# RWKV passes: TensorE products from the gram to the last inverse level as tiles of 32 columns in place of 64

## The chip, the cores and the metric

The kernel runs on one core of one Trainium2 chip. The metric is the device time in microseconds. The kernel before takes 2187.87 us (median of two runs, 2187.61 and 2188.13).

The core's engines are PE (TensorE; PEld is its weight load), DVE (VectorE), ACT (ScalarE), POOL (GpSimd) and SP, which issues DMAs.

## What is computed

Two blocks follow each other on 512 tokens of width 1024, all in float32. The first mixes a gated convolution and a forgetting attention and ends in a feed-forward part. The second puts 16 meta tokens ahead (528 tokens), runs an RWKV-7 mixer and then a latent attention. The change lies in the RWKV mixer:

```python
r, k, v, g, w_lo, a_lo = jnp.split(h, ...)            # h = [x, dx] @ w_comb, 32 heads of 64
def step(S, inp):
    r_t, w_t, k_t, v_t, a_t, b_t = inp
    sa = jnp.einsum('bhij,bhj->bhi', S, a_t)
    S = S * w_t[:, :, None, :] + sa[..., None] * b_t[:, :, None, :] + v_t[..., None] * k_t[:, :, None, :]
    return S, jnp.einsum('bhij,bhj->bhi', S, r_t)
```

The recurrence over tokens is not run token by token: it is cut into chunks of 64 tokens, and within a chunk a unit triangular system is solved.

## The kernel before

The 32 heads are worked off as 16 pairs (`PAIRS`); the two heads of a pair lie on partitions 0 to 63 and 64 to 127 (`own[0]`, `own[1]`). The tokens, padded to 576, make 9 chunks (`NC_`) of `C` = 64. A pass `i` is a software pipeline over three pairs:

- A, pair `i`: the projections of r, k, v and g. Each of 8 items (four kinds by two token halves of 264) is 8 steps (`KD`) of a contraction over 1024 channels; a step is one `fill`. It issues one product for each of the two column halves `own` of the pair: weights `raw_k` of 128 rows x 64 columns, 264 streamed columns, into two halves of the partitions of a PSUM bank (L1446).
- B, pair `b = i - 1`: the gram products (L1650, weights of 64 rows x 128 columns) and the inverse of the triangular systems of the nine chunks, by squaring in levels 1 to 5. A level makes x = mb' t (L1661, `x_mm`), which DVE evicts to `x_m` (L2036), and then t' = t x (L1677, at the last level L1679, `tt_mm`), which DVE adds to `t_m` (L2042). Each product of a chunk streams 64 columns against 64 weight columns for each of the two heads. The chunks go in two parts (4 and 5, or 3 and 5 from level 4 on), so that DVE works on one while PE works on the other.
- C, pair `c = i - 2`: the scan over the chunks (L1569 to L1621).

Beside these, `head_sums` (L1707) sums squares over a head's 64 channels with a matrix of ones: four products of 264 streamed columns, called in the inverse by `ssk` (level 3) and `gn_var` (level 4) and behind it by `bonus`.

The order on each engine is written out by hand. On PE, `fill(k)` draws the next k projection steps between the dependent products, by the tables `FILL_GRAM` = 7, `FILL_FIRST` = 5, `FILL_X` = (2, 2, 2, 2, 2) and `FILL_T` = (2, 2, 1, 0, 1): 28 steps from the gram to the end of the inverse. Passes with an inverse are i = 1 to 16; those with projections are i = 0 to 15. In pass 16 the fills are steps of the output projection instead (`wo_unit`, L161 to L163, weights of 128 x 128).

Of the kernel before, what the change touches and what calls it, by code (L numbers as in the profile page):

```python
# [37 lines left out]
C = 64  # L38
# [32 lines left out]
def program(nc, io, out):  # L71
    with ExitStack() as base:
# [27 lines left out]
        ps = base.enter_context(nc.psum_tensor("ps", [P, 8, 512], F32))  # L100
# [1220 lines left out]
        mb = put("mb", [P, NC_, P])  # L1321
        tb = put("tb", [P, NC_, P])
        rb = put("rb", [P, NC_, P])
        t_m = put("t_m", [P, NC_, C])
        x_m = put("x_m", [P, NC_, 2, C])
        t_t = put("t_t", [P, NC_, C])
# [55 lines left out]
        def parts_of(lv):  # L1382
            return PARTS if lv < 4 else LAST_PARTS
        own = [slice(C * h, C * h + C) for h in range(2)]

        SCAN_FILLS = [(1, 2, 2), (1, 1, 1)] + [(1, 1, 2)] * (NC_ - 3) + [(1, 1, 2)]
        FILL_TURN, FILL_GRAM, FILL_FIRST, FILL_END = 1, 7, 5, 0
# [8 lines left out]
        def ge(eng, s, v):  # L1396

            if not (isinstance(v, int) and v <= 0):
                eng.wait_ge(s, v)
# [21 lines left out]
        def item_out(n):  # L1421
            bank, at = ITEM_AT[n]
            return ps[:, bank, at:at + T2 // 2]
# [5 lines left out]
        def projection(pe, i, n):  # L1429

            kind, h = ITEMS[n]
            dst = item_out(n)
            t = "rkvg".index(kind)
            cols = slice(h * (T2 // 2), (h + 1) * (T2 // 2))
            before = [m for m in range(n) if ITEM_AT[m][0] == h]
            if before:
                pe.wait_ge(a_ev, 12 * i + (before[-1] + 1))
            else:
                ge(pe, a_ev, 12 * i - 1)
            if h == 0:  # L1440
                pe.wait_ge(rw_landed[t % 2], 32 * i + (16 * (t // 2) + 16))
            for k in range(KD):
                if i == 0 and h == 0:
                    pe.wait_ge(mx_done, KD * t + k + 1)
                for m in own:
                    mm = nc.tensor.matmul(dst[m, :], raw_k[t % 2][:, k, m], mixed[t][:, k, cols], start=(k == 0), stop=(k == KD - 1))  # L1446
                if k == KD - 1:

                    mm.then_inc(a_mm, 1)
                yield  # L1450
# [96 lines left out]
        def pass_pe(pe, i, A, B, Cs):  # L1547
# [10 lines left out]
            def fill(k):  # L1558

                for _ in range(k):  # L1560
                    next(steps, None)
# [11 lines left out]
            def p_product(n):  # L1573

                for h in range(2):
                    mm = nc.tensor.matmul(ps[own[h], 2, 0:C], gm[:, n, 1, own[h]], uv[:, n, h, :], start=True, stop=True)  # L1576
                mm.then_inc(p_mm, 1)
            if Cs:
                pe.wait_ge(rb_ev, 2 * c + 2)
            for n in range(NC_):  # L1580
# [24 lines left out]
                if Cs:  # L1605
                    pe.wait_ge(p_ev, 9 * c + (n + 1))
                    for h in range(2):
                        mm = nc.tensor.matmul(ps[own[h], 2, C:P], tb[:, n, own[h]], p_sb[:], start=True, stop=True)  # L1608
# [4 lines left out]
                if Cs:  # L1613
# [5 lines left out]
                    if n < NC_ - 1:  # L1619
                        for h in range(2):  # L1620
                            mm = nc.tensor.matmul(ps[own[h], 3, C:P], bk_rows[:, n, own[h]], uv[:, n, h, :], start=(n == 0), stop=True)  # L1621
# [6 lines left out]
            if B:  # L1628

                pe.wait_ge(fa, 14 * b + FA["v"])  # L1630
                pe.wait_ge(pa, 13 * b + PA["bkb"])
                if A:
                    pe.wait_ge(a_ev, 12 * i + LORA)
                else:
                    for x in range(NC_):
                        if x % 8 == 0:
                            pe.wait_ge(yy_ev, 2 * c + (x // 8 + 1))
                        for h in range(2):
                            mm = nc.tensor.matmul(ps[own[1 - h], 5 + x // 8, C * (x % 8):C * (x % 8) + C], rkv[:, x, 2 * C:3 * C],
                                                  cent[:, own[h]], start=True, stop=True)  # L1640
                    mm.then_inc(turn_mm, 1)
                fill(fill_turn)
                if not A:
                    pe.wait_ge(rows_turned, TURNED * b + (NC_ - 1 + 2))
                elif Cs:
                    pe.wait_ge(yy_ev, 2 * c + 2)
                for q, (c0, m) in enumerate(TURNS):
                    for x in range(m):
                        for h in range(2):
                            mm = nc.tensor.matmul(ps[:, 2 + 3 * h + q, x * P:x * P + P], bk[own[h], c0 + x, :],  # L1650
                                                  rkv[own[h], c0 + x, 0:2 * C], start=True, stop=True)
                    mm.then_inc(g_mm, 1)
                fill(fill_gram)
                for lv in range(1, 6):
                    for p, (c0, m) in enumerate(parts_of(lv)):
                        if lv == 1:
                            pe.wait_ge(mb_ev, 4 * b + (2 * p + 2))
                        pe.wait_ge(tm_ev if lv == 1 else tadd_ev, 2 * b + (p + 1) if lv == 1 else 8 * b + (2 * (lv - 2) + p + 1))
                        for x in range(m):
                            for h in range(2):  # L1660
                                mm = nc.tensor.matmul(ps[own[h], 2 + p, x * C:x * C + C], mb[:, c0 + x, own[h]], t_m[:, c0 + x, :],  # L1661
                                                      start=True, stop=True)
                        mm.then_inc(x_mm, 1)
                        if lv == 1 and p == 0:
                            fill(fill_first)
                    fill(fill_x[lv - 1])
                    for p, (c0, m) in enumerate(parts_of(lv)):
                        pe.wait_ge(x_ev, 10 * b + (2 * (lv - 1) + p + 1))
                        if lv == 1:
                            pe.wait_ge(t0_ev, 6 * b + (2, 6)[p])  # L1670
                        else:
                            pe.wait_ge(tb_ev, 8 * b + (2 * (lv - 2) + p + 1))
                        for x in range(m):
                            for h in range(2):
                                dst = ps[own[h], 4 + p, x * C:x * C + C]
                                if lv < 5:
                                    mm = nc.tensor.matmul(dst, t_t[:, c0 + x, :], x_m[:, c0 + x, h, :], start=True, stop=True)  # L1677
                                else:
                                    mm = nc.tensor.matmul(dst, x_m[:, c0 + x, h, :], t_t[:, c0 + x, :], start=True, stop=True)  # L1679
                        mm.then_inc(tt_mm, 1)  # L1680
                    fill(fill_t[lv - 1])
                    if lv == 3 and A:
                        ssk(pe, i)
                    if lv == 4 and Cs:
                        gn_var(pe, i, c, A)
                pe.wait_ge(kkgm_ev, 2 * b + 2)
                pe.wait_ge(state0, 4 * b + (4 if A else 2))
                p_product(0)
                if A:
                    bonus(pe, i, Cs, c)  # L1690
                fill(fill_end)
            else:
                fill(25 if A else 8)
                if A:
                    ssk(pe, i)
                    fill(8)
                if Cs:
                    pe.wait_ge(wo_ev, 2 * EARLY)
                    gn_var(pe, i, c, A)
                    fill(16)  # L1700
                if A:
                    bonus(pe, i, Cs, c)

        def head_sums(src):
            for h in range(2):
                for m in own:
                    mm = nc.tensor.matmul(ps[m, 6 + h, 0:T2 // 2], halves_ones[:, m], src(h), start=True, stop=True)  # L1707
            return mm

        def ssk(pe, i):  # L1710
            pe.wait_ge(fa, 14 * i + FA["sq"])
            head_sums(lambda h: token_cols(sq_b, h)).then_inc(ssk_mm, 1)

        def gn_var(pe, i, c, A):
            pe.wait_ge(ysq_ev, c + 1)
            if A:
                pe.wait_ge(ssk_out, i + 1)
            head_sums(lambda h: ysq_b[:, h * (T2 // 2):(h + 1) * (T2 // 2)]).then_inc(var_mm, 1)

        def bonus(pe, i, Cs, c):  # L1720
            pe.wait_ge(pa, 13 * i + PA["rr"])
            if Cs:
                pe.wait_ge(gn_ln, c + 1)
            else:
                pe.wait_ge(ssk_out, i + 1)
            head_sums(lambda h: token_cols(rr_b, h)).then_inc(bon_mm, 1)
# [1193 lines left out]
        with nc.Block() as block:  # L2920
# [77 lines left out]
            def _(pe):  # L2998
                front_pe(pe)
                all_passes(pe, pass_pe, x2_under=False)  # L3000
                def squares_of(slot, h):
                    at, cols = HALVES2[h]
# [290 lines left out]
```

## Time and profile before

| | us |
|---|---|
| median of the runs | 2187.87 |
| span of the profiled execution | 2182.5 |
| PE busy | 2151.9 (99%) |
| PE weight load busy | 1730.7 (79%) |
| DVE / POOL / ACT busy | 1287.0 (59%) / 1199.3 (55%) / 829.3 (38%) |
| L1446 (projections), four kinds | 146.5 + 144.0 + 137.6 + 125.4 |
| L1661 (x of the inverse) | 96.9 |
| L1677 (t of the inverse) | 77.3 |

The profile is of one execution. Its span goes from the first to the last instruction; the time of a run also takes in what lies around it. A record of PE is a MATMUL instruction from the start of its reading to a modelled end, so records overlap and their mean duration is not what each adds to the time: for that, read where one run of records starts and where the next does. A form such as "128*64 128x264 f32" is rows*columns of the weights and partitions x elements streamed.

### The profile page before, as it was taken

The numbers are of one execution on the slowest core, as the hardware profiler recorded it, in microseconds if no ns is written. First come the engines' busy times: TensorE is split into PE (matmuls) and PEld (weight loads), VectorE is DVE, ScalarE is ACT, GpSimd is POOL, SyncE is SP. The second block draws the span as 40 slices with busy tenths as digits, with TensorE's granted clock in tenths as the row PEclk, the third lists the DMA queues.
The fourth block names the chain that finished last, engine by engine and source line by source line (L and its number), as shares of the span: only waits on it lengthen the run. The fifth ranks groups of instructions, "written<-read, shape, count | busy, mean of one in ns | idle before, by whom it ended". The sixth has DMA issues, their size and how long they took to land.

```text
span 2182.5 us, 49885 instructions
## 1 busy us (share of the span) xinstructions
PE 2151.9 (99%) x20695; PEld 1730.7 (79%) x20695; DVE 1287.0 (59%) x2558; ACT 829.3 (38%) x1712; POOL 1199.3 (55%) x843
## 2 busy tenths in 40 slices
PE   8999999999999999999999999999989999999999
PEld 6888888788888767777777777777879788888877
DVE  5465467977850766666666666666531476656521
ACT  4122212333320354555555555555411345444410
POOL 5555567788766163555545555555636443443455
PEclk9999999999999999999999999999999999999999
DMA  4323323333332143333333333333624322212132
GB/s 130 87 77 85 80 88 96 93 98 98 98 108 97 42 124 77 87 95 89 90 93 98 90 101 105 90 90 90 196 71 125 107 69 63 66 53 57 54 127 95
DMA packets 368490, 200.80 MB, mean 92 GB/s; under 512 B 124411, under 2 KB 348793, under 8 KB 367881
## 3 DMA queue, kind: packets, MB, share of 16 engines
q1 hardware_dynamic: 368074, 197.53, 32.3%
q8 instruction: 166, 2.72, 0.5%
q14 instruction: 59, 0.48, 0.1%
q10 hardware_dynamic: 191, 0.07, 0.0%
HBM read 162.69 MB, written 22.04 MB: 85 GB/s over the span
## 4 chain that ended last, share of the span: by engine, by line
PE 92%; DVE 3%; POOL 2%; ACT 1%; issue 1%; DMA 0%; SPq 0%; DVEq 0%; POOLq 0%; ACTq 0%
PE ps L1446 21%; PE ps L161 16%; PE ps L163 16%; PE ps L162 16%; PE ps L1661 4%; PE ps L1677 3%; PE ps L1707 2%; PE ps L1650 2%; PE ps L2722 2%; PE ps L1621 1%; PE ps L1576 1%; PE ps L1608 1%; PE ps L1569 1%; PE ps L2706 1%; PE ps L1464 1%
## 5 line engine op out<-in xcount | busy, mean ns | idle before, releaser
L152 POOL TENSOR_TENSOR w_lo<-raw,w_hi 128x1024 fp32r<-128x1024 f32 (+1 forms) x163 | 416.6, 2556 | 13.6
L149 POOL TENSOR_SCALAR w_hi<-raw 128x1024 fp32r<-128x1024 f32 (+1 forms) x163 | 182.2, 1118 | 397.1 <-PE ps L163 380.9
L161 PE MATMUL ps<-h_hi,w_hi 128*128 128x512 f32 x616 | 242.2, 393 | 2.8 <-DVE h_lo L1129 1.7
L163 PE MATMUL ps<-h_hi,w_lo 128*128 128x512 f32 x616 | 240.0, 390 | 0.0
L162 PE MATMUL ps<-h_lo,w_hi 128*128 128x512 f32 x616 | 239.9, 389 | 0.0
L1446 PE MATMUL ps<-mixed_k,raw 128*64 128x264 f32 x1024 | 146.5, 387 | 0.0
L1446 PE MATMUL ps<-mixed_r,raw 128*64 128x264 f32 x1024 | 144.0, 387 | 0.2 <-ACT ws_b L1741 0.2
L161 PEld LDWEIGHTS ps<-h_hi,w_hi 128*128 128x128 f32 x616 | 115.7, 188 | 28.6 <-DVE h_lo L1129 2.8
L1446 PE MATMUL ps<-mixed_g,raw 128*64 128x264 f32 x1024 | 137.6, 387 | 0.0
L163 PEld LDWEIGHTS ps<-h_hi,w_lo 128*128 128x128 f32 x616 | 115.7, 188 | 24.5
L162 PEld LDWEIGHTS ps<-h_lo,w_hi 128*128 128x128 f32 x616 | 115.8, 188 | 22.9
L1144 DVE SCALAR_TENSOR_TENSOR up_c<-up_raw,params,up_c 128x512 f32<-128x512 f32 x88 | 119.0, 1357 | 20.3 <-ACT up_c L862 18.7
L1446 PE MATMUL ps<-mixed_v,raw 128*64 128x264 f32 x1024 | 125.4, 388 | 0.0
L2036 DVE TENSOR_TENSOR x_m<-ps,lv_pad 128x640 f32<-128x640 f32 (+2 forms) x160 | 110.8, 726 | 16.4 <-PE ps L1661 11.9
L1661 PEld LDWEIGHTS ps<-t_m,mb 128*64 128x64 f32 x2752 | 96.1, 138 | 15.2 <-DVE t_m L2042 0.4
L1661 PE MATMUL ps<-t_m,mb 128*64 128x64 f32 x2752 | 96.9, 222 | 0.2 <-DVE t_m L2042 0.2
L1446 PEld LDWEIGHTS ps<-mixed_v,raw 128*64 128x64 f32 x1024 | 71.0, 137 | 31.4
L1979 DVE COPY uv<-ps 64x64 f32<-64x64 f32 x160 | 34.8, 218 | 94.6 <-PE ps L1608 94.1
L161 PE MATMUL ps<-z_both,w_hi 128*128 128x264 f32 x256 | 80.7, 315 | 6.9 <-POOL w_lo L2095 5.9
L2827 ACT ACTIVATE xT<-ps,nmax 128x144 f32<-128x144 f32 (+1 forms) x64 | 34.6, 541 | 135.6 <-DVE nmax L2865 135.4
L1677 PEld LDWEIGHTS ps<-x_m,t_t 128*64 128x64 f32 x2240 | 76.7, 138 | 10.5 <-DVE x_m L2036 0.6
L1758 ACT ACTIVATE uv<-ps 64x64 f32<-64x64 f32 x128 | 27.9, 218 | 146.7 <-PE ps L1608 146.7
(494 smaller groups left out, 5823.5 us busy)
## 6 DMA issues: line engine op xcount, KB each, us to landing
raw<-in_rwkv_w_in_dram SPq DMA_DIRECT2D x64, 512.0 KB, 4.4
raw<-in_w_up_dram SPq DMA_DIRECT2D x44, 512.0 KB, 3.9
raw<-in_w_in_dram SPq DMA_DIRECT2D x41, 512.0 KB, 3.9
raw<-in_w_down_dram SPq DMA_DIRECT2D x22, 512.0 KB, 3.5
raw<-in_mla_w_in_dram SPq DMA_DIRECT2D x22, 512.0 KB, 4.0
sb_kept<-xT SPq DMA_DIRECT2D x16, 528.0 KB, 2.7
xT<-sb_kept SPq DMA_DIRECT2D x16, 528.0 KB, 4.5
raw<-in_rwkv_w_out_dram SPq DMA_DIRECT2D x16, 512.0 KB, 4.4
```

What stands on the lines that cost most here:

```text
L149: nc.gpsimd.tensor_scalar(w_hi[s][:, 0:width], raw[s][:, 0:width], 1.0, 0.0, ALU.mult, ALU.add).then_inc(split_hi, 1)
L152: nc.gpsimd.tensor_tensor(w_lo[s][:, 0:width], raw[s][:, 0:width], w_hi[s][:, 0:width].bitcast(F32), ALU.subtract).then_inc(split_ready, 1)
L161: nc.tensor.matmul(dst, w[0], x[0], start=start, stop=False)
L162: nc.tensor.matmul(dst, w[0], x[1], start=False, stop=False)
L163: return nc.tensor.matmul(dst, w[1], x[0], start=False, stop=stop)
L1144: nc.vector.scalar_tensor_tensor(out=up_c[:, ab, 1 + k, :], in0=up_raw[:, n % 4, 1 - k:1 - k + T1], scalar=prm(("cf1", "cf0")[k], n // 2 + ...
L1446: mm = nc.tensor.matmul(dst[m, :], raw_k[t % 2][:, k, m], mixed[t][:, k, cols], start=(k == 0), stop=(k == KD - 1))
L1650: mm = nc.tensor.matmul(ps[:, 2 + 3 * h + q, x * P:x * P + P], bk[own[h], c0 + x, :], rkv[own[h], c0 + x, 0:2 * C], start=True, stop=True)
L1661: mm = nc.tensor.matmul(ps[own[h], 2 + p, x * C:x * C + C], mb[:, c0 + x, own[h]], t_m[:, c0 + x, :], start=True, stop=True)
L1677: mm = nc.tensor.matmul(dst, t_t[:, c0 + x, :], x_m[:, c0 + x, h, :], start=True, stop=True)
L1707: mm = nc.tensor.matmul(ps[m, 6 + h, 0:T2 // 2], halves_ones[:, m], src(h), start=True, stop=True)
L2036: nc.vector.tensor_tensor(x_m[:, c0:c0 + m, :, :], part_of(2 + p, m).unsqueeze(2).to_broadcast([P, m, 2, C]), lv_pad[:, lv - 1, :, :].unsq ...
```

## The change

From behind the gram's products to behind the last inverse level, everything that was issued as two column tiles of 64 is issued as four of 32 (`quads`): both sorts of inverse products, the projection steps drawn by `fill`, and the head sums of `ssk` and `gn_var`. `col_tiles[0]` holds the tiling in force; `fill` and `head_sums` read it. For the t products the weights are `t_t` or `x_m`, whose 64 columns are cut in two (`of`), and the head is `n // 2`. The scan, the gram and `bonus` keep their tiles. Nothing is moved on any other engine, and the semaphores are incremented by the last product of each run as before.

```diff
         own = [slice(C * h, C * h + C) for h in range(2)]
+        quads = [slice(32 * q, 32 * q + 32) for q in range(4)]
+        col_tiles = [own]
...
-                for m in own:
+                for m in col_tiles[0]:
                     mm = nc.tensor.matmul(dst[m, :], raw_k[t % 2][:, k, m], mixed[t][:, k, cols], start=(k == 0), stop=(k == KD - 1))
...
                     mm.then_inc(g_mm, 1)
+                col_tiles[0] = quads
                 fill(fill_gram)
...
-                            for h in range(2):
-                                mm = nc.tensor.matmul(ps[own[h], 2 + p, x * C:x * C + C], mb[:, c0 + x, own[h]], t_m[:, c0 + x, :],
+                            for q in quads:
+                                mm = nc.tensor.matmul(ps[q, 2 + p, x * C:x * C + C], mb[:, c0 + x, q], t_m[:, c0 + x, :],
                                                       start=True, stop=True)
...
-                            for h in range(2):
-                                dst = ps[own[h], 4 + p, x * C:x * C + C]
+                            for n, q in enumerate(quads):
+                                dst, h, of = ps[q, 4 + p, x * C:x * C + C], n // 2, quads[n % 2]
                                 if lv < 5:
-                                    mm = nc.tensor.matmul(dst, t_t[:, c0 + x, :], x_m[:, c0 + x, h, :], start=True, stop=True)
+                                    mm = nc.tensor.matmul(dst, t_t[:, c0 + x, of], x_m[:, c0 + x, h, :], start=True, stop=True)
                                 else:
-                                    mm = nc.tensor.matmul(dst, x_m[:, c0 + x, h, :], t_t[:, c0 + x, :], start=True, stop=True)
+                                    mm = nc.tensor.matmul(dst, x_m[:, c0 + x, h, of], t_t[:, c0 + x, :], start=True, stop=True)
...
                         gn_var(pe, i, c, A)
+                col_tiles[0] = own
                 pe.wait_ge(kkgm_ev, 2 * b + 2)
...
             for h in range(2):
-                for m in own:
+                for m in col_tiles[0]:
                     mm = nc.tensor.matmul(ps[m, 6 + h, 0:T2 // 2], halves_ones[:, m], src(h), start=True, stop=True)
```

On PE, from the gram to the second inverse product of level 1 of one pass, the kernel before issues the following (weights are columns x streamed columns; the row of L1650 is the gram, L1446 are projection steps):

```order
L1650 MATMUL ps<-rkv,bk 128x128 x18
L1446 MATMUL ps<-mixed_v,raw 64x264 x14
L1661 MATMUL ps<-t_m,mb 64x64 x8
L1446 MATMUL ps<-mixed_v,raw 64x264 x10
L1661 MATMUL ps<-t_m,mb 64x64 x10
L1446 MATMUL ps<-mixed_g,raw 64x264 x4
L1677 MATMUL ps<-x_m,t_t 64x64 x18
```

At the same place the changed kernel issues this (its lines are numbered two or more higher):

```order
L1652 MATMUL ps<-rkv,bk 128x128 x18
L1448 MATMUL ps<-mixed_v,raw 32x264 x28
L1664 MATMUL ps<-t_m,mb 32x64 x16
L1448 MATMUL ps<-mixed_v,raw 32x264 x20
L1664 MATMUL ps<-t_m,mb 32x64 x20
L1448 MATMUL ps<-mixed_g,raw 32x264 x8
L1680 MATMUL ps<-x_m,t_t 32x64 x36
```

Nothing has changed its place; each run behind the gram has twice the products, of half the weight columns.

At the end of the inverse on PE the kernel before stands so (L1707 is `gn_var` with xT, then `bonus` with rr_b):

```order
L1707 MATMUL ps<-xT,halves_ones 64x264 x4
L1661 MATMUL ps<-t_m,mb 64x64 x16
L1446 MATMUL ps<-mixed_g,raw 64x264 x4
L1679 MATMUL ps<-t_t,x_m 64x64 x16
L1446 MATMUL ps<-mixed_g,raw 64x264 x2
L1576 MATMUL ps<-uv,gm 64x64 x2
L1707 MATMUL ps<-rr_b,halves_ones 64x264 x4
```

and the changed one so:

```order
L1711 MATMUL ps<-xT,halves_ones 32x264 x8
L1664 MATMUL ps<-t_m,mb 32x64 x32
L1448 MATMUL ps<-mixed_g,raw 32x264 x8
L1682 MATMUL ps<-t_t,x_m 32x64 x32
L1448 MATMUL ps<-mixed_g,raw 32x264 x4
L1578 MATMUL ps<-uv,gm 64x64 x2
L1711 MATMUL ps<-rr_b,halves_ones 64x264 x4
```

Ahead of L1578 (L1576 before) the tile's columns now change from 32 to 64. In the whole program the products on PE go from 13493 to 17205.

## Rows read from the trace of the kernel before

**Rows 1.** The page: busy time by engine, instruction blocks, and the chain.

```profile
PE 2151.9 (99%) x20695; PEld 1730.7 (79%) x20695; DVE 1287.0 (59%) x2558; ACT 829.3 (38%) x1712; POOL 1199.3 (55%) x843
...
q8 instruction: 166, 2.72, 0.5%
...
PE 92%; DVE 3%; POOL 2%; ACT 1%; issue 1%; DMA 0%; SPq 0%; DVEq 0%; POOLq 0%; ACTq 0%
```

**Rows 2.** Timeline of PE: start us, us, engine, line, out<-in, form, records.

```profile
279.32 1.09 PE L520 MATMUL ps<-a_pT,v_rows 128*64 128x128 f32 x16
280.35 0.50 PE L161 MATMUL ps<-at_hi,w_hi 128*128 128x512 f32 x1
...
1003.72 2.05 PE L1650 MATMUL ps<-rkv,bk 64*128 64x128 f32 x31
...
1014.31 1.06 PE L1446 MATMUL ps<-mixed_g,raw 128*64 128x264 f32 x8
1015.20 1.22 PE L1661 MATMUL ps<-t_m,mb 128*64 128x64 f32 x36
1016.25 1.06 PE L1446 MATMUL ps<-mixed_g,raw 128*64 128x264 f32 x8
...
1023.40 1.10 PE L1661 MATMUL ps<-t_m,mb 128*64 128x64 f32 x32
1024.34 1.06 PE L1446 MATMUL ps<-mixed_g,raw 128*64 128x264 f32 x8
1025.23 1.15 PE L1677 MATMUL ps<-x_m,t_t 128*64 128x64 f32 x32
1026.21 1.06 PE L1707 MATMUL ps<-xT,halves_ones 128*64 128x264 f32 x8
...
1028.93 1.13 PE L1679 MATMUL ps<-t_t,x_m 128*64 128x64 f32 x32
1029.88 0.62 PE L1446 MATMUL ps<-mixed_g,raw 128*64 128x264 f32 x4
1030.33 0.28 PE L1576 MATMUL ps<-uv,gm 128*64 128x64 f32 x4
...
1054.99 2.28 PE L1650 MATMUL ps<-rkv,bk 64*128 64x128 f32 x36
```

**Rows 3.** Busy time by engine in the stretch of one pass, clock, DMA.

```profile
1005.93:1030.33 24.40, 24.40 (x474) 19.34 (x474) 20.57 (x45) 13.80 (x22) 11.02 (x10) 1.00 0.21 42
```

**Rows 4.** Groups by line: form, records | busy us, mean ns | idle before.

```profile
L161 PEld LDWEIGHTS ps<-h_hi,w_hi 128*128 128x128 f32 x616 | 115.7, 188 | 28.6 <-DVE h_lo L1129 2.8
L1446 PE MATMUL ps<-mixed_v,raw 128*64 128x264 f32 x1024 | 125.4, 388 | 0.0
L1661 PEld LDWEIGHTS ps<-t_m,mb 128*64 128x64 f32 x2752 | 96.1, 138 | 15.2 <-DVE t_m L2042 0.4
L1661 PE MATMUL ps<-t_m,mb 128*64 128x64 f32 x2752 | 96.9, 222 | 0.2 <-DVE t_m L2042 0.2
```

**Rows 5.** Timeline of PE in the last pass with an inverse.

```profile
1582.31 0.28 PE L162 MATMUL ps<-z_both,w_hi 128*128 128x264 f32 x1
1582.43 0.28 PE L163 MATMUL ps<-z_both,w_lo 128*128 128x264 f32 x1
1582.64 1.27 PE L1677 MATMUL ps<-x_m,t_t 128*64 128x64 f32 x36
1583.84 0.39 PE L161 MATMUL ps<-z_both,w_hi 128*128 128x264 f32 x1
1584.07 0.28 PE L162 MATMUL ps<-z_both,w_hi 128*128 128x264 f32 x1
```

**Rows 6.** Waits in PE's sequencer: ns min/median/max, first and last start us.

```profile
L1606 PEldq EVENT_SEMAPHORE  x1: 51/51/51, 1031.6 to 1031.6; - x1
L1618 PEldq EVENT_SEMAPHORE  x1: 51/51/51, 1031.7 to 1031.7; - x1
```

## Prediction

> **What bounds the kernel now.** I read the page first. Matrix multiplies are on record for 99% of the span, VectorE for 59%, and the chain that ended last lies on PE for 92% [rows 1]. PE's busy time is modelled, so I looked at where each run of products starts. In a pass of the RWKV part (timeline of PE, [rows 2]) one run starts as soon as the run before has been streamed, and the same pieces recur in every pass. The stretch that the change touches runs from behind the gram (L1650, line numbers of before throughout) to L1576: 1005.93 to 1030.33 us, 24.4 us, in which PE is busy all the time, VectorE for 20.6 us, at granted clock 1.00, that is 2.4 GHz [rows 3]. There are 16 such stretches, so about 390 of 2182.5 us are touched and every ns there is on the path. What a product costs is therefore its start-to-start distance, not the 222 or 387 ns of one record [rows 4].
>
> How the distance is made up: an f32 product leaves two MATMUL records (1376 products on L1661, 2752 records). The two halves of 64 columns stand in different column tiles. Four records of 264 columns (a pair of products) take 0.89 us / 2 = 0.445 us: from 1014.31 to 1015.20 are 8 records [rows 2]. At two cycles of 2.4 GHz a column one record streams 220 ns; two pairs of records need 440 ns if the two tiles of a pair stream side by side, 880 ns if not. So they do stream side by side, and a pair of records costs 222.5 ns, its streaming and 2.5 ns more. I call the records that stream together (one for each tile) a group. With 64 streamed columns 36 records, 18 groups, go from 1015.20 to 1016.25: 58.2 ns a group, against 53.3 ns of streaming, 4.9 ns more. L520 has the same 64-column weights with 128 streamed columns: 8 groups from 279.32 to 280.35, 1.03 us, less about 0.15 us for changing the tile shape (below), is 110 ns, against 106.7: about 3 ns more. So the longer excess shows only where streaming is as short as the weight load. Weight loads of 128 and of 64 columns last 188 and 138 ns [rows 4], 0.78 ns a column, so 64 columns load in 50 ns: with the load starting just after the group before it, the load and not the stream sets the 58.2 ns.
>
> **The change, part by part.**
>
> *More instructions, same columns.* Each product of 64 weight columns becomes two of 32. By the order of the program 3712 more products are issued on PE (2752 for the inverse on L1661, L1677, L1679, 840 projection steps on L1446, 120 head sums on L1707), 7424 more MATMUL records and as many loads. The streamed columns for one tile are unchanged; what changes is that a group has four records.
>
> *Inverse products.* A pass has 86 products of a chunk (43 of L1661, 35 of L1677, 8 of L1679), each two groups: 172 groups; 2752 in 16 passes. If four tiles stream side by side as two do, a group costs 53.3 ns and the excess. The load of 32 columns is about 25 ns by 0.78 ns a column (an estimate from the two durations), hidden behind the stream, so I take the excess of the 264-column rows, 2.5 ns: 55.8 ns. That saves 2.4 ns x 172 = 0.41 us a pass. Bounds: below, nothing under 53.3 ns is possible, 4.9 ns x 2752 = 13.5 us saved at the very most; above, no row of before has four column tiles, so the far end is that only two of four stream together (a rival, below).
>
> *Projection steps and head sums in the stretch.* 28 fill steps a pass (x15) and two head sums (x15): 1920 records of 64 columns before, 960 groups, each 222.5 ns and already stream-bound. Four records of 32 columns: the same 222.5 ns. Zero, as long as four stream together.
>
> *Who gains from it.* At the end of the stretch PE already waits a little on VectorE: L1677 at 1025.23 takes 0.98 us for 32 records where L1661 at 1023.40 takes 0.94, L1679 at 1028.93 takes 0.95. There a faster PE is met by the same VectorE chain (20.6 of 24.4 us busy), so I give back 0.04 us a pass: 0.37 us x 15 = 5.5 us. The pass without a projection (from 1571 us) waits on VectorE for much of its inverse; I count 0.2 us.
>
> *One more change of shape a pass.* Behind the gram a change of tile shape happened anyway (64 rows x 128 columns to 128 x 64). New is the step from 32 back to 64 columns before L1576, once a pass. Its price stands in the last pass, where products of 128 columns lie between those of 64 [rows 5]: L1677 with 36 records takes 1.20 us from 1582.64 to 1583.84, 0.15 us over the 1.05 of [rows 2]; the records of 128 columns just before and behind stand 0.21 and 0.23 us from the next, where their neighbours stand 0.12. That is 0.35 us for in and out, 0.15 to 0.18 for one. I take 0.15, since a load of 32 or 64 columns refills sooner than one of 128: +2.4 us.
>
> *Can PE be fed?* With four tiles a group of the inverse is 8 instructions in 55.8 ns, 7.0 ns each; before it was 14.5. The sequencer passed the wait of L1606 at 1031.6 and that of L1618 at 1031.7 [rows 6]: at most 0.2 us apart, with two waits of 51 ns begun, one of them inside, and six products, 24 instructions, between. That is (200 - 51) / 24 = 6.2 ns at most. A run of 72 records is 144 instructions and two waits: at most 144 x 6.2 + 102 = 995 ns against 1005 ns of streaming. It suffices, by little at this bound. Instruction blocks: 166 blocks for 2.72 MB [rows 1] become some 224; 176 instructions in 1.9 us of the inverse make one for every 2.8 us, where 88 in 1.94 us made one for every 5.6.
>
> **Sum.** 2182.5 - 5.5 - 0.2 + 2.4 = 2179.2 us in the profiled execution. That one lies 5.4 us under the median of 2187.87, which covers what lies around its span, so 2184.6 us.
>
> A rule speaks against this sum. The only mean spacing that rows show is 29.1 ns a matrix multiply (1.05 us / 36 records), and none is denser; within a group the partner starts without its own stream time, but that is a single pair. Whether a sustained 14 ns is possible no row of before shows. The Trainium skill's page "TensorE: Matmul & The Clock Gate" (Part 1, on the issue floor) says that start-to-start never falls below some 25 ns however few columns are streamed; by that figure a group of four would be 100 ns and the whole 115 us slower, an estimate from that page. Its Part 3 says that tiles run side by side and start about 4 ns apart, which points the other way. What the rows make of either is in the rivals.
>
> **Rivals.**
>
> 1. *An issue floor for each matrix multiply.* If the 29.1 ns is a floor and not half of a 58.2 ns stream, four records cost 116.4 ns, 58.2 more for each of 2752 groups: 160 us, so 2187.9 + 160 + 2.4 = 2350 us, slower. Projection groups (four in 222.5 ns) would be untouched. It decides as soon as the floor is over 18.5 ns (2752 x (4 x 18.5 - 58.2) ns is 43 us, 2%). Against it: 6.2 ns an instruction at the sequencer is 12.4 ns for a load and its multiply. For it: no denser row.
>
> 2. *Only two column tiles stream together.* Then both kinds double: 160 us and 960 x 222.5 ns = 214 us: about 2562 us. Against it: pairs of column tiles and pairs of row tiles show no loss at all; for it: no row has four.
>
> 3. *A small price for each added tile.* If the excess grows with the tiles (2.5 ns each: 63.3 ns a group, 5 ns more), or the feed just misses (loads of four tiles late, instruction blocks late at one for every 2.8 us, VectorE's semaphores later by the fourth tile), the loss is 5 to 15 ns a group: 14 to 41 us, 2192 to 2231 us. For it: the feed bound above has 10 ns to spare in 1005.
>
> 4. *No effect at all* of the narrower load: groups stay at 58.2 ns, and the change of shape costs 2.4 us: 2190.3 us.
>
> **How the numbers follow.** Forecast 0.55 (own range 2180 to 2187), rival 4 0.13, rival 3 0.14, rival 1 0.10, rival 2 0.07, and 0.01 for a gain over 2%, for which I see no mechanism. Under 2% is about what a measurement of this kernel can't tell from no change. So: faster 0.01, same 0.82, slower 0.17. The low end is 2179: an excess of 1 ns in place of 2.5 (1.5 ns x 2752 = 4.1 us), and 1.4 us less for give-back and shape; to leave out no more than 2 in 10 the range takes in rival 4 and most of rival 3: up to 2220. I predict 2184.6 us.
>
> **What would show it.** In the profile after: 36 + 36 records of 64 streamed columns take about 1.00 us (1.05 now, 2.1 under rival 1 or 2); 16 records of 264 columns take 0.89 us (1.78 under rival 2 alone); loads of 32 columns last about 112 ns; between the last record of 32 columns and L1576's second group some 0.15 us are added; from gram to gram 51.05 us where it was 51.27 (1003.72 to 1054.99, [rows 2]). The prediction is wrong if the inverse runs are longer than 1.05 us while the projection runs are not (issue or feed), or if PE's sequencer shows waits for instructions.

## The result, and the profile after

The changed kernel takes 2268.32 us (2266.21 to 2270.43, two runs) where the kernel before takes 2187.87: the ratio is 1.037, 95% interval 1.035 to 1.039. It is 80 us slower; 2184.6 us was forecast, with 2220 as the upper end of the range.

The page of the profile after: span, PE, instruction blocks, and the chain that ended last.

```profile
span 2264.5 us, 64733 instructions
PE 2174.8 (96%) x28119; PEld 1743.1 (77%) x28119; DVE 1289.4 (57%) x2558; ACT 829.5 (37%) x1712; POOL 1199.4 (53%) x843
q8 instruction: 224, 3.67, 0.7%
q14 instruction: 59, 0.48, 0.1%
PE 91%; issue 3%; DVE 3%; POOL 2%; ACT 1%; DMA 0%; SPq 0%; DVEq 0%; POOLq 0%; ACTq 0%
```

The other engines are busy for as long as in [rows 1]. PE lost 3% of its share, and the chain has three times the "issue": time in which PE waited for nothing that the profile shows. The PE waits of the kernel after say on which lines (us in total, times, longest):

```profile
PE ps L1680 <- issue: 23.8, 21, 3.3
PE ps L1664 <- issue: 23.2, 27, 1.8
PE ps L1448 <- issue: 6.6, 9, 1.8
...
PE ps L1682 <- issue: 3.6, 6, 0.9
PE ps L1711 <- issue: 1.7, 5, 0.5
```

These are the inverse's products and what lies between them. 59 us are shown as idle. The modelled ends hide a further 0.2 us of each gap, since a record is drawn 220 ns long where the next one starts after 14. Read from start to start and with the smallest ones, the gaps of the 16 passes come to some 78 us, so nearly the whole loss lies in them. Timeline of PE after, in the pass that answers to [rows 2] (its gram begins at 1024.76):

```profile
1026.97 3.32 PE L1448 MATMUL ps<-mixed_v,raw 128*32 128x264 f32 x56
...
1034.22 1.19 PE L1680 MATMUL ps<-x_m,t_t 128*32 128x64 f32 x72
1035.23 1.07 PE L1448 MATMUL ps<-mixed_g,raw 128*32 128x264 f32 x16
1036.12 0.89 PE L1664 MATMUL ps<-t_m,mb 128*32 128x64 f32 x49
1037.22 0.48 PE L1664 MATMUL ps<-t_m,mb 128*32 128x64 f32 x20 [0.21 <-issue]
...
1042.37 1.21 PE L1664 MATMUL ps<-t_m,mb 128*32 128x64 f32 x72 [1.83 <-issue]
1043.37 1.10 PE L1448 MATMUL ps<-mixed_g,raw 128*32 128x264 f32 x16
1044.26 0.76 PE L1680 MATMUL ps<-x_m,t_t 128*32 128x64 f32 x39
1045.99 0.66 PE L1680 MATMUL ps<-x_m,t_t 128*32 128x64 f32 x33 [0.97 <-issue]
...
1056.07 0.34 PE L1578 MATMUL ps<-uv,gm 128*64 128x64 f32 x4
```

Three things are to be read here. First, tiles of 32 columns do what was forecast while they run: 72 records of the inverse take 1.01 us (1034.22 to 1035.23; 36 records took 1.05 in [rows 2]), and 16 records of projection 0.89 us (1035.23 to 1036.12), as 8 did. Second, PE then stands still in the middle of a run (after 39 of 72 records), where no semaphore is waited for. Third, between the two restarts at 1042.37 and 1045.99 lie 72 + 16 + 39 = 127 MATMUL records; with their weight loads that is 254 instructions, and the two waits on that way (one for each part of level 3's t products) make 256. The other three intervals between restarts of this pass (at 1037.22, 1042.37, 1045.99, 1049.46 and 1053.28) count out the same way: 127, 128 and 127 records, with two, no and two waits. Over all passes 57 restarts follow the one before them after 126 to 128 records. That is the size of an instruction block: the change adds 14848 instructions (64733 less 49885) and 58 blocks (224 less 166), 256 to a block. Blocks are 16.4 KB each (3.67 MB / 224), and the two instruction queues together move 4.15 MB for 64733 instructions, 64 bytes each. The stretch takes 29.1 us (1026.97 to 1056.07) instead of 24.4.

Theory F, formed from this and still to be tested: PE's instructions come in blocks of 256; the next block is fetched only when the one before it has been entered, and takes some 3.5 us to be there. Where PE gets through 256 instructions in less, it waits out the rest. The change doubles PE's instructions while the work for the array is the same: 88 instructions in 1.94 us become 176 in 1.9 us, so a block lasts 2.8 us. The rivals are L, a price for each added record; P, that PE can't keep up one multiply in 14 ns for long; T, that the blocks are late only because other transfers are in their way.

### The profile page after: what moved, and what is told of

The parts are those of the page before. It is cut to its first block, busy times and chain, and to the rows that moved or that the text cites. A ratio compares the mean times of both kernels' runs of the same rounds, so it can differ in the third digit from the quotient of the medians.

```text
span 2264.5 us, 64733 instructions
## 1 busy us (share of the span) xinstructions
PE 2174.8 (96%) x28119; PEld 1743.1 (77%) x28119; DVE 1289.4 (57%) x2558; ACT 829.5 (37%) x1712; POOL 1199.4 (53%) x843
## 3 DMA queue, kind: packets, MB, share of 16 engines
q8 instruction: 224, 3.67, 0.7%
## 4 chain that ended last, share of the span: by engine, by line
PE 91%; issue 3%; DVE 3%; POOL 2%; ACT 1%; DMA 0%; SPq 0%; DVEq 0%; POOLq 0%; ACTq 0%
PE ps L1448 20%; PE ps L161 16%; PE ps L162 15%; PE ps L163 15%; PE ps L1664 4%; PE ps L1680 3%; PE ps L1711 2%; PE ps L1652 2%; PE ps L2726 1%; PE ps L1578 1%; PE ps L1623 1%; PE ps L1610 1%; PE ps L1571 1%; PE ps L1682 1%; PE ps L2710 1%
## 5 line engine op out<-in xcount | busy, mean ns | idle before, releaser
L152 POOL TENSOR_TENSOR w_lo<-raw,w_hi 128x1024 fp32r<-128x1024 f32 (+1 forms) x163 | 416.1, 2553 | 13.6
L1448 PE MATMUL ps<-mixed_g,raw 128*32 128x264 f32 (+1 forms) x1984 | 152.7, 388 | 6.9 <-issue 6.6
L1664 PEld LDWEIGHTS ps<-t_m,mb 128*32 128x32 f32 x5504 | 99.5, 110 | 41.0 <-issue 28.0
L1664 PE MATMUL ps<-t_m,mb 128*32 128x64 f32 x5504 | 106.8, 220 | 23.5 <-issue 23.2
L1448 PE MATMUL ps<-mixed_v,raw 128*32 128x264 f32 (+1 forms) x1744 | 125.3, 387 | 0.0
L1680 PE MATMUL ps<-x_m,t_t 128*32 128x64 f32 x4480 | 85.7, 221 | 24.2 <-issue 23.8
L1680 PEld LDWEIGHTS ps<-x_m,t_t 128*32 128x32 f32 x4480 | 80.2, 111 | 35.0 <-issue 27.5
L2108 POOL TENSOR_TENSOR kk_sq<-kk_sq,xT 128x528 f32<-128x528 f32 x16 | 21.2, 1323 | 148.6 <-ACT xT L1855 148.5
L1448 PEld LDWEIGHTS ps<-mixed_v,raw 128*32 128x32 f32 (+1 forms) x1744 | 66.1, 115 | 35.4
L1448 PEld LDWEIGHTS ps<-mixed_g,raw 128*32 128x32 f32 (+1 forms) x1984 | 71.8, 111 | 25.5 <-issue 11.9
```

Source lines behind the costliest of these rows:

```text
L152: nc.gpsimd.tensor_tensor(w_lo[s][:, 0:width], raw[s][:, 0:width], w_hi[s][:, 0:width].bitcast(F32), ALU.subtract).then_inc(split_ready, 1)
L1664: mm = nc.tensor.matmul(ps[q, 2 + p, x * C:x * C + C], mb[:, c0 + x, q], t_m[:, c0 + x, :], start=True, stop=True)
L1680: mm = nc.tensor.matmul(dst, t_t[:, c0 + x, of], x_m[:, c0 + x, h, :], start=True, stop=True)
```

## Experiments

### The fetch by itself

A kernel with nothing but long rows of multiplies on constant tiles, each row on a line of its own. The rows that matter:

```python
for n in range(512):                    # L47: written out, 2048 instructions
    nc.tensor.matmul(ps[q4(n), 1, 0:64], w[:, q4(n)], x[:, 0:64], start=True, stop=True)
...
for n in range(512):                    # L51: tiles of 64 columns
    nc.tensor.matmul(ps[q2(n), 2, 0:64], w[:, q2(n)], x[:, 0:64], start=True, stop=True)
...
with nc.Fori(0, 32, engines=(mybir.EngineType.PE,)) as _:
    for n in range(32):                 # L68: 128 instructions, run 32 times
        nc.tensor.matmul(ps[q4(n), 6, 0:64], w[:, q4(n)], x[:, 0:64], start=True, stop=True)
```

> Not the reference's computation: long rows of matrix multiplies on constant tiles alone, no data transfers meanwhile, zeros as output. Each section is over a thousand PE instructions. Theory F, at 3.5 us a block of 256 instructions, 13.7 ns an instruction, four instructions for an f32 product: L47 (512 products, 32 weight columns, 64 streamed, written out): 28 us, with gaps of some 1.7 us a block apart, where the stream alone would take 14.3 us (27.9 ns a product); L55 (32 x 96): 28 us for 21 us of stream; L59 (32 x 128): 28 us, at the edge; L51 (64 x 64): 29.8 us, its stream, no gap; L63 (bf16, 64 x 128, two instructions a product): 14.9 us, its stream. L68 is L47's section as a loop of 32 products run 32 times, whose 128 instructions stay in the buffer: 1024 x 27.9 ns = 28.6 us and a few us for the loop's own instructions, so half of L47's time for a product. Theory P (PE itself cannot keep 14 ns a record up for long): L68 is as slow for a product as L47, and no gap stands a block apart. Theory T (the blocks are late only because data transfers are in their way): without transfers L47 takes 14.3 us.

Groups of PE of this kernel (form, records | busy us, mean ns | idle before), and the chain within L47 (start us, us):

```profile
L68 PE MATMUL ps<-x,w 128*32 128x64 f32 x2048 | 33.9, 220 | 0.0
L51 PE MATMUL ps<-x,w 128*64 128x64 f32 x1024 | 30.0, 222 | 0.0
L59 PE MATMUL ps<-x,w 128*32 128x128 f32 x1024 | 28.2, 273 | 0.0
L55 PE MATMUL ps<-x,w 128*32 128x96 f32 x1024 | 22.8, 247 | 4.2 <-issue 4.2
L47 PE MATMUL ps<-x,w 128*32 128x64 f32 x1024 | 15.9, 220 | 10.9 <-issue 10.9
L63 PE MATMUL ps<-xb,wb 128*64 128x128 bf16 x512 | 14.5, 219 | 0.0
```

```profile
64.93 1.99 PE ps L47 x128
66.92 2.01 issue
68.94 1.99 PE ps L47 x128
70.92 1.74 issue
72.66 1.99 PE ps L47 x128
74.65 1.46 issue
76.12 1.99 PE ps L47 x128
78.11 1.74 issue
79.85 1.99 PE ps L47 x128
81.84 1.46 issue
83.30 1.99 PE ps L47 x128
```

L47 runs 128 records, 256 instructions, and then stands still; from block to block it takes 4.01, 3.72, 3.46, 3.73 and 3.45 us. Its whole row took 15.9 + 10.9 = 26.8 us where the stream takes 14.3. L55 streams half as much again and takes the same time (27.0 us), L59 twice as much and takes 28.2: below some 3.5 us a block the array's work does not matter. L55's blocks too stand 3.45 to 3.73 us apart. L51, the tiles of before, and L63 have no gap. The same products from a loop (L68) have none either: 33.1 ns a product where L47 has 52.3. That is more than the 27.9 expected; the 32 rounds cost 5.3 us together, 0.16 us a round, which I put down to the loop's own instructions without having measured them. Theory P is out, and so is T as the only cause: there were no other transfers.

The trace also shows the fetches themselves. Over 64 to 84 us, in slices of half a microsecond:

```profile
GB/s 0 0 0 0 33 0 0 0 0 0 0 0 33 0 0 0 0 0 0 33 0 0 0 0 0 0 33 0 0 0 0 0 0 33 0 0 0 0 0 0
q8 instruction: 5, 0.08, 1.8%
```

Each block is one packet of 16 KB on the instruction queue. By the trace's records the five packets start at 66.07, 70.07, 73.70, 77.15 and 80.94 us, each 1.0 to 1.15 us after a restart of PE; each moves for 0.9 to 1.5 us, and PE restarts 1.4 to 1.55 us after its end. So one block is under way at a time, and it is asked for only when PE has entered the block before: this is F's mechanism, seen and not only inferred. Over the loop L68 (338.5 to 371.0 us) the trace has no packet on any queue.

> The same rows of multiplies, with loads of 2 MB from HBM one after the other all along (90 of them, 4 KB and less a packet). Not the reference's computation. Theory F: sections as in the quiet kernel, a block taking somewhat longer (the 16 DMA engines serve both), up to 4 us, so L47 28 to 33 us; L68 unchanged at its 28.6 us and the loop's instructions. Theory T: L47 14.3 us in the quiet kernel and clearly more here.

The page of this kernel for the transfers, its groups of PE, and its timeline in L47:

```profile
q1 hardware_dynamic: 94176, 190.85, 93.6%
```

```profile
L51 PE MATMUL ps<-x,w 128*64 128x64 f32 x1024 | 34.4, 233 | 13.6 <-issue 13.6
L68 PE MATMUL ps<-x,w 128*32 128x64 f32 x2048 | 33.9, 221 | 0.0
L47 PE MATMUL ps<-x,w 128*32 128x64 f32 x1024 | 23.0, 270 | 20.9 <-issue 20.9
```

```profile
75.06 3.20 PE L47 MATMUL ps<-x,w 128*32 128x64 f32 x128 [2.56 <-issue]
80.43 3.11 PE L47 MATMUL ps<-x,w 128*32 128x64 f32 x128 [2.17 <-issue]
85.80 1.99 PE L47 MATMUL ps<-x,w 128*32 128x64 f32 x128 [2.27 <-issue]
92.00 1.29 PE L47 MATMUL ps<-x,w 128*32 128x64 f32 x40 [4.21 <-issue]
```

With the DMA engines busy for 93.6% of the time, a block takes 5.4 to 6.2 us in these lines, and 4.8 to 7.0 us (6.2 in the median) over all rows of this kernel that stall. I had expected 4 at most. What grows is the time until the instruction packet starts: 2.5 to 4.7 us after the restart, where it was 1.0 to 1.2 in the quiet kernel. From its end to the next restart it is 1.2 to 1.6 us in both. Even the tiles of 64 columns (L51) now lose 13.6 us, and the loop nothing, though the loads run beside it too. So T has a part: other transfers lengthen the time of a block. Part of L47's own time here is the array at a lower granted clock (0.946 over this kernel, 0.996 in the quiet one): the 128 records from 75.06 and those from 80.43 us last 3.2 and 3.1 us at a mean granted clock of 0.59 and 0.60, so for most of it at 1.2 GHz; those from 85.80 us last 1.99 at 1.00, 2.4 GHz.

### Spread in the full kernel: levels in a row, or every other one

Both keep every result. In the first, tiles of 32 columns are in force in levels 1 to 3, in the second in levels 1, 3 and 5: 54 and 52 of 86 products, the same work in another place.

```diff
+                    if lv == LAST_QUADS + 1:
+                        col_tiles[0] = own
...
-                            for q in quads:
+                            for q in (quads if lv <= LAST_QUADS else own):
```

Here `LAST_QUADS` is 3. The kernel with levels 1, 3 and 5:

```diff
                 for lv in range(1, 6):
+                    col_tiles[0] = quads if lv % 2 else own
...
-                            for q in quads:
+                            for q in (quads if lv % 2 else own):
```

The t products are switched by the same conditions.

> Tiles of 32 columns in levels 1, 2 and 3, of 64 behind it; every result is computed. 54 of 86 chunk products in tiles of 32 columns, as many as in the kernel with levels 1, 3 and 5, but in a row, with one change of shape. Theory F: stalls a block apart from level 2 on, about 43 us slower than before, 2231 us, so 20 us slower than the one with levels 1, 3 and 5, although that has four more changes of shape a pass. Theory L: 0.63 x 80 = 50 us, about 2238 us, and faster than the one with levels 1, 3 and 5.

> Tiles of 32 columns in levels 1, 3 and 5, of 64 in levels 2 and 4 (projection steps with their level); every result is computed. 52 of 86 chunk products in tiles of 32 columns, five changes of shape a pass instead of one. Theory F: the dense runs of some 360 instructions are parted by levels at the old rate, in which the next block catches up, so 15 us for the changes of shape and under 10 us of stalls, about 2208 us. Theory L (a price for each added record): 0.60 x 80 = 48 us and 11 us for the changes, about 2247 us.

Levels 1 to 3: 2234.94 us (2230.97 to 2238.91), ratio 1.022 (1.017 to 1.026). Levels 1, 3 and 5: 2204.90 us (2204.33 to 2205.48), ratio 1.008 (1.005 to 1.011). So 30 us lie between two kernels with nearly the same records, and the one with four more changes of tile shape a pass is the faster. Theory L had the order the other way round. The first kernel's time alone decides nothing: its two runs lie 8 us apart and take in both forecasts, 2231 and 2238. PE's waits, of levels 1 to 3 first:

```profile
PE ps L1685 <- issue: 18.7, 15, 2.3
PE ps L1667 <- issue: 12.2, 14, 2.0
```

```profile
PE ps L1683 <- issue: 4.2, 3, 2.0
```

That fits F: a run of 360 instructions at the fast rate is mostly over before the second block boundary hurts, if a slow level comes behind it. The count of stalls shows it; no run varies the length of the fast runs alone.

### The first level, and the first two

> Tiles of 32 columns from the gram to the end of level 1 only; every result is computed. 18 of 86 chunk products in tiles of 32 columns, one change of shape more a pass (16 x 0.19 = 3 us by the kernel with two levels), 36 groups a pass 2.4 ns cheaper (1.4 us). Theory F: the dense part is shorter than a block, no stall, 2 to 5 us slower than before, about 2191 us. Theory L: 0.21 x 80 = 17 us slower, about 2205 us.

Measured: 2189.91 us (eight runs, 2186.94 to 2193.80), ratio 1.0014 (1.0003 to 1.0025). L's 2205 is out, and F's 2191 is met. But F's reason, no stall at all, is not quite right:

```profile
PE ps L1685 <- issue: 2.4, 4, 1.1
```

Three of the 16 passes still stall at the end of level 1's t products (at 1428.65, 1480.52 and 1532.83 us). The fourth gap, 0.32 us at 1545.01, lies in level 4, in tiles of 64, where loads keep the DMA engines full (384 GB/s from 1538 to 1545 us).

> Tiles of 32 columns from the gram to the end of inverse level 2 only, 64 behind it; every result is computed. Theory F (instruction blocks: a block of 256 PE instructions needs about 3.5 us from the request to its use, only one is under way, and PE stands still where it consumes 256 instructions faster): the dense part is only 72 of 172 groups of the inverse and starts with a full buffer, so 0 to 2 short stalls a pass, 5 to 20 us slower than before, about 2198 us; the first idle time that no engine explains lies in level 2. Theory L (a price for each added record of 32 columns, 80 us spread evenly over the groups of the inverse): 0.42 x 80 = 34 us slower, about 2222 us.

Measured: 2213.63 us, ratio 1.012 (1.009 to 1.015): 26 us slower. That lies between both expectations, so by itself it tells nothing; the number of stalls was underrated. With level 1 (+3), levels 1 to 3 (+48) and all five (+80) the series shows no even price: the first level costs 3 us, each later one 16 to 23 us.

### One kind of product at a time

The first kernel leaves out the line `col_tiles[0] = quads`, so only the inverse is in tiles of 32; the second puts `own` in place of `quads` in both inverse loops, so only the projections and head sums are.

> All inverse products in tiles of 32 columns, projection steps and head sums between them in tiles of 64; every result is computed. About 22 changes of tile shape a pass at 0.145 us. Theory F: 160 PE instructions per level half in about 2.2 us are one block for every 3.5 us, so hardly a stall: 16 x 22 x 0.145 = 51 us slower for the changes, 6 us faster for the inverse runs, about 2233 us, and faster than the changed kernel in spite of the changes of shape. Theory L (the loss sits in the inverse records): 51 + 80 us slower, about 2318 us.

> Projection steps and head sums of the stretch in tiles of 32 columns, inverse products in tiles of 64; every result is computed. The same 22 changes of tile shape a pass. Theory F: 104 instructions in about 2.3 us, one block for 5.6 us, no stall at all: 51 us slower than before, about 2239 us. If changes of shape between 32 and 64 columns are cheaper than between 64 and 128, both kernels of this kind come out lower by the same amount.

Measured: 2245.39 us (ratio 1.027, 1.024 to 1.030) and 2234.93 us (1.022, 1.019 to 1.025). The first is faster than the changed kernel by 23 us, although it changes the tile shape 22 times in the stretch of a pass where the other does once; L had it 50 us slower. Timeline of PE, the inverse in tiles of 32:

```profile
1033.34 1.07 PE L1448 MATMUL ps<-mixed_g,raw 128*32 128x264 f32 x16
```

is the changed kernel's piece, and these are of the first kernel:

```profile
1032.98 1.11 PE L1448 MATMUL ps<-mixed_g,raw 128*64 128x264 f32 x8
1034.02 1.32 PE L1679 MATMUL ps<-x_m,t_t 128*32 128x64 f32 x72
1035.27 1.11 PE L1448 MATMUL ps<-mixed_g,raw 128*64 128x264 f32 x8
1036.31 1.21 PE L1663 MATMUL ps<-t_m,mb 128*32 128x64 f32 x72
1038.01 1.11 PE L1448 MATMUL ps<-mixed_g,raw 128*64 128x264 f32 x8 [0.49 <-issue]
```

The changed kernel's run of projection takes 0.89 us to the next start, here it takes 1.04: 0.15 us for a change of shape, which is the size forecast from [rows 5]. In the second kernel no gap without a reason is left in the inverse:

```profile
1029.80 1.27 PE L1664 MATMUL ps<-t_m,mb 128*64 128x64 f32 x36
1031.00 1.10 PE L1448 MATMUL ps<-mixed_g,raw 128*32 128x264 f32 x16
1032.03 1.27 PE L1682 MATMUL ps<-x_m,t_t 128*64 128x64 f32 x36
```

The inverse's run takes 1.20 us to the next start and the projection's 1.03, against 1.05 and 0.89 without a change. The 49 us over the runs of before beside it (2185.82 us) are thus accounted for by the changes of shape: 23 in each of the 15 passes with projections, 0.14 us each. The first kernel keeps twelve gaps in the inverse (8.6 us), since 160 instructions in 2.3 us (1034.02 to 1036.31) make a block of 3.7 us, at the edge (22 changes a pass).

## Why the prediction failed, and what held

**What bounds the kernel**: held. PE is the path, and what it loses is lost one to one: the pass shown is 4.7 us longer in the stretch.

**Four tiles stream together, at 55.8 ns a group**: held: 1.005 us for 18 groups in the trace, as forecast. Rivals 1 (an issue floor), 2 (two tiles at a time) and 4 (no effect) fall with the same row. Here hangs the rule that spoke against the sum: the Trainium skill's "TensorE: Matmul & The Clock Gate" (Part 1) has some 25 ns from start to start whatever the columns. The trace does not agree: 72 f32 records of tiles of 32 columns stand 14.0 ns apart on the mean.

**Projection steps at no price**: held, 0.89 us for a pair of steps.

**A change of shape at 0.15 us**: held (0.14 and 0.15 us in the two kernels above).

**Can PE be fed?** This is the step that failed. It had two parts. The sequencer's bound (6.2 ns an instruction) was enough: 144 instructions went by in 1.005 us, 7.0 ns each. The other part counted the instruction blocks, found one for every 2.8 us where there had been one for every 5.6, and put no duration beside it. The term that was left out is the time from one block to the next: 3.45 to 4.01 us with no other transfers, against 2.8 us of work. The step gave the fetch a share in rival 3 and capped it at 41 us with a price for each group, as if it were spread evenly. It is not: it is nothing for the first block or so and then 0.7 to 1.2 us for each, and more beside loads, once PE is faster than the fetch. The low end of rival 3, 2192 us, does not follow from its own 14 us either: 2187.9 + 14 + 2.4 is 2204. In the pass shown the chain of waits has five gaps, 0.21, 1.83, 0.97, 0.15 and 0.76 us. The 1.83 is more than the difference of 3.5 and 2.8 us gives; there the block's packet starts only at 1040.00 us, 2.78 us after the restart at 1037.22, when 540 KB of loads have just gone through. This recurs: of the 57 restarts that follow another by one block, 47 have under 100 KB of loads between them and come 3.3 to 4.3 us apart; the seven with over 400 KB come 4.5 to 6.7 us apart, their packets starting 2.0 to 4.1 us after the restart instead of 1.05 to 1.7. Together with the kernel with loads this puts the long gaps down to loads in the block's way.

Could it have been seen? The trace of before has no gap of this kind, and its instruction blocks stood in the page. What no row of before gave is the time a block takes, since PE never ran out. That is an unknown resource whose demand the change doubles: it should have been a rival of its own, with a price from the one thing known, that the densest demand so far had been met, and none beyond.

**The sum again.** 16 passes: -6.6 us at most for the inverse runs, +2.4 us for one change of shape, and the rest, some 84 us or 5.3 us a pass. The gaps in the trace give some 78 of these; the other 6 are not shown anywhere in particular. No version tried beats the kernel before: with level 1 alone, which hardly stalls, 36 groups at 2.4 ns save 0.09 us a pass and the change of shape takes 0.15.

## What to carry to other kernels

Count the instructions of an engine against the time that they cover, not only the work in them. On PE a written-out stretch that gets through 256 instructions (64 f32 products) in under about 3.5 us stalled here, from the second or third block boundary on. Up to 4 us it was at the edge, and with the DMA engines full of loads even 3.7 us stalled at every boundary but the first; narrower tiles, smaller products and f32's two records all push that way. A short dense run between slower ones is nearly safe. Idle time that the profile puts down to "issue" and that recurs every 256 instructions is this, and the packets of the instruction queue confirm it.

## What the runs showed of the hardware that I had not expected

- A block of 256 instructions takes PE 3.45 to 4.01 us from the last with no other transfers, 4.8 to 7.0 us with the DMA engines 94% busy. In both cases PE restarts 1.2 to 1.6 us after the end of the block's packet; loads delay the packet's start. At that load even the tiles of 64 columns, at 14.6 ns an instruction, lost 13.6 us of 48.
- The fetch looks ahead by one block only: in the quiet kernel's stalling rows each block's packet starts 1.0 to 1.2 us after PE has restarted with the block before.
- A loop of 128 instructions on PE is served without fetching, with no packet on the instruction queue in 32.5 us of it: 33.1 ns a product where the same products written out take 52.3 ns.
- With streaming longer than the weight load, a group of four column tiles costs its stream and 2.5 ns, the same as a group of two.
